# Turning the normalised latent rows with VectorE and DMAs instead of TensorE in a hybrid decoder layer

## The reference

```python
h = x @ w_in[l]
(qa, ka, va, ga, iq, ik, iw, c_q, c_kv, k_rope, gb) = _split_cols(h)
# A: rope(qa), rope(ka); indexer scores from iq, ik, iw pick 128 keys per query; softmax over these
o_a = _dsa_branch(qa, ka, va, iq, ik, iw) * jax.nn.silu(ga)
# B: latent attention; c_q has 256 columns, c_kv has 128
q  = _rmsnorm(c_q,  q_norm_g)  @ w_uq     # 8 heads of 64 + 32 rotary columns
kv = _rmsnorm(c_kv, kv_norm_g) @ w_ukv    # 8 heads of 64 key + 64 value columns
o_b = softmax(causal(q_nope k_nope + q_pe k_pe)) v * jax.nn.silu(gb)
out = jnp.concatenate([o_a, o_b], axis=-1) @ w_out[l]
x = _layernorm(DEEPNORM_ALPHA * x + out, ln_g[l], ln_b[l])
```

## Time and profile before

| | us |
|---|---|
| median of 3 runs | 284.46 (283.82 to 284.49) |
| the profiled execution | 284.04 |
| its span, from first to last instruction | 282.2 |
| TensorE busy | 273.8 (97%) |
| VectorE busy | 232.2 (82%) |
| GpSimd busy | 188.6 (67%) |
| ScalarE busy | 149.6 (53%) |
| mean granted clock of TensorE | 0.991 |

### The profile page before, as it was taken

The page is one execution under the profiler, slowest core; times in us unless marked ns, Lnnn a source line. Parts: engine busy times, 40 slices in busy tenths (PEclk is TensorE's granted clock), DMA queues, the critical chain, the costliest instruction groups (busy, mean ns, idle before and its releaser), DMA issues.

```text
span 282.2 us, 5134 instructions
## 1 busy us (share of the span) xinstructions
PE 273.8 (97%) x1664; PEld 228.6 (81%) x1664; DVE 232.2 (82%) x528; ACT 149.6 (53%) x352; POOL 188.6 (67%) x209
## 2 busy tenths in 40 slices
PE   8999999999999999999999999999999999999990
PEld 7999987778888888888888888885778788888890
DVE  2699998989999999999984798668694967986375
ACT  5656534674452576224188696777764774552000
POOL 5898999834199999999935993885799923010012
PEclk9999999999999999999999999999999999999996
DMA  7985543222623396221238652817800000545022
GB/s 240 364 256 172 151 138 130 74 77 74 149 59 93 83 250 190 74 74 44 70 91 211 231 141 78 224 53 270 349 2 2 0 1 2 172 110 168 0 77 74
DMA packets 20874, 35.41 MB, mean 125 GB/s; under 512 B 6928, under 2 KB 9488, under 8 KB 20592
## 3 DMA queue, kind: packets, MB, share of 16 engines
q1 hardware_dynamic: 20272, 34.79, 41.0%
q10 hardware_dynamic: 576, 0.29, 0.4%
HBM read 26.69 MB, written 2.10 MB: 102 GB/s over the span
## 4 chain that ended last, share of the span: by engine, by line
PE 96%; DMA 1%; DVE 1%; DVEq 0%; issue 0%; ACT 0%
PE ps L1320 52%; PE ps L1643 16%; PE ps L1560 6%; PE ps L1521 5%; PE ps L1581 3%; PE ps L1605 3%; PE ps L1503 2%; PE ps L1336 2%; PE ps L1506 2%; PE ps L1430 2%; DMA w_raw<-in_w_in 1%; PE ps L1540 1%; PE ps L1616 1%; PE ps L1439 0%; PE ps L1413 0%; DVEq L255 0%
## 5 line engine op out<-in xcount | busy, mean ns | idle before, releaser
L624 POOL TENSOR_TENSOR w_lo<-w_raw,w_hi 128x512 fp32r<-128x512 f32 (+3 forms) x62 | 83.8, 1374 | 17.4 <-ACT w_hi L770 16.8
L770 ACT ACTIVATE w_hi<-w_raw 128x512 fp32r<-128x512 f32 (+3 forms) x62 | 35.9, 595 | 55.2 <-PE ps L1320 51.9
L881 ACT ACTIVATE probs<-probs,small 128x512 f32<-128x512 f32 (+3 forms) x64 | 35.7, 559 | 23.2 <-DVE small L1150 22.8
L1643 PE MATMUL ps<-wo_hi,oT 128*128 128x512 f32 (+1 forms) x144 | 45.4, 388 | 0.0
L1320 PE MATMUL ps<-w_hi,x_lo 128*128 128x512 f32 (+3 forms) x120 | 43.0, 362 | 0.0
L1320 PE MATMUL ps<-w_lo,x_hi 128*128 128x512 f32 (+3 forms) x120 | 42.9, 361 | 0.0
L1320 PE MATMUL ps<-x_hi,w_hi 128*128 128x512 f32 x96 | 38.0, 396 | 0.0
L1320 PE MATMUL ps<-x_lo,w_hi 128*128 128x512 f32 x96 | 37.4, 390 | 0.0
L1320 PE MATMUL ps<-x_hi,w_lo 128*128 128x512 f32 x96 | 37.4, 389 | 0.0
L1320 PE MATMUL ps<-w_hi,x_hi 128*128 128x512 f32 (+2 forms) x84 | 32.1, 382 | 0.0
L1643 PEld LDWEIGHTS ps<-wo_hi,oT 128*128 128x128 f32 x144 | 25.9, 189 | 5.2 <-issue 0.2
(11 more groups left out here) (196 smaller groups left out, 631.3 us busy)
## 6 DMA issues: line engine op xcount, KB each, us to landing
w_raw<-in_w_in SPq DMA_DIRECT2D x20, 512.0 KB, 3.6
kaT_swap<-kaT SPq DMA_DIRECT2D x8, 256.0 KB, 3.8
w_raw<-in_w_out SPq DMA_DIRECT2D x4, 512.0 KB, 4.8
wo_early<-in_w_out SPq DMA_DIRECT2D x4, 512.0 KB, 4.8
wo_raw_b<-in_w_out SPq DMA_DIRECT2D x4, 512.0 KB, 4.8
x_res<-in_x SPq DMA_DIRECT2D x4, 512.0 KB, 7.1
x_raw<-in_xT SPq DMA_DIRECT2D x3, 512.0 KB, 6.4
out_y<-y SPq DMA_DIRECT2D x6, 256.0 KB, 2.4
```

Source lines behind the costliest of these rows:

```text
L624: pool.tensor_tensor(w_lo[:, s, 0:n], w_raw[:, s, 0:n], w_hi[:, s, 0:n], ALU.subtract).then_inc(w_lo_ready, 1)
L770: act.activation(dst, w_raw[:, s, 0:n], ACT.Copy).then_inc(w_hi_ready, 1)
L881: act.activation(probs[:, u % NPROBS, 0:N], probs[:, u % NPROBS, 0:N], ACT.Exp, bias=neg_max[:, u % 8:u % 8 + 1], scale=-1.0, accum_out=ro ...
L1643: ins = mm(out_ps(i, b), oT[i % 2][:, o, k, :], w[:, wcols], start=first, stop=final)
```

## The change

VectorE turns the normalised rows in 32x32 blocks, four instructions (one for 128 rows, 384 columns) after the indexer's scores and ahead of the reduction of the rotary angles, into `lat_st`. SyncE, after load 21, waits for them and issues sixteen DMAs that set the blocks in place in `lat_pT`: each takes 32 partitions to 32 partitions, with twelve runs of 128 bytes on each at the destination. TensorE's twelve transposes and their waits go. ScalarE's latT_hi and VectorE's latT_lo read `lat_pT` in SBUF where they read PSUM; latT_hi waits for the sixteen DMAs. GA's evacuation now waits for the last logits and the four turns, and TensorE's QPE for latT_hi and latT_lo. Both new tiles lie in SBUF where the raw x was.

```diff
+    lat_st = sb("lat_st", 102, [P, 4, QL_T + 1, TT, SQ])
+    lat_pT = sb("lat_pT", 108, [P, QL_T + 1, TT, 4, SQ])
...
+        def latT_raw(t):
+
+            return lat_pT[:, t].rearrange("p m a q -> p (m a q)")
...
                 load(q)
...
+                if q == LAT_PLACE_AT:
+                    sp.wait_ge(lat_turned, TT)
+                    for c in range(4):
+                        for a in range(4):
+                            sp.dma_start(lat_pT[SQ * c:SQ * (c + 1), :, :, a], lat_st[SQ * a:SQ * (a + 1), c]).then_inc(lat_placed, 16)
...
-                    act.wait_ge(side_ready, F_LAT + QL_T + 1)
+                    act.wait_ge(side_ready, F_END)
+                    act.wait_ge(lat_turned, TT)
...
             def evac_lat_hi():
                 act.wait_ge(norm_g_loaded, 32)
+                act.wait_ge(lat_placed, 16 * 16)
                 for t in range(QL_T + 1):
-                    n = F_LAT + t
-                    act.wait_ge(side_ready, n + 1)
-                    act.activation(latT_hi[:, t, :], side[:, n % 4], ACT.Copy,
+                    act.activation(latT_hi[:, t, :], latT_raw(t), ACT.Copy,
                                    scale=gq[:, t:t + 1] if t < QL_T else gkv).then_inc(lat_hi_ready, 1)
...
             dve.wait_ge(relu_used, (TT - 1) * IDX_HEADS)
 
+            dve.wait_ge(lat_normed, 2 * TT)
+            for m in range(TT):
+                V.transpose(lat_st[:, :, :, m].rearrange("p c t q -> p t c q"),
+                            lat_tok[:, m, 0:Q_LORA + KV_LORA].rearrange("p (t c q) -> p t c q", c=4, q=SQ)).then_inc(lat_turned, 1)
+
             dve.wait_ge(dve_step, rows_turns)
             reduce_angle(ang_rows[:, :], turns_rows[:, :], rows_arg_ready)
...
             for t in range(QL_T + 1):
-                n = F_LAT + t
                 dve.wait_ge(lat_hi_ready, t + 1)
-                V.scalar_tensor_tensor(out=latT_lo[:, t, :], in0=side[:, n % 4], scalar=gq[:, t:t + 1] if t < QL_T else gkv,
-                                       in1=latT_hi[:, t, :], op0=ALU.mult, op1=ALU.subtract).then_inc(side_read[n % 4], 2)
+                V.scalar_tensor_tensor(out=latT_lo[:, t, :], in0=latT_raw(t), scalar=gq[:, t:t + 1] if t < QL_T else gkv,
+                                       in1=latT_hi[:, t, :], op0=ALU.mult, op1=ALU.subtract).then_inc(lat_lo_ready, 1)
...
-            def lat_transposes():
-                pe.wait_ge(lat_normed, 2 * TT)
-                for t in range(QL_T + 1):
-                    bank = fill(F_LAT + t)
-                    for m in range(TT):
-                        ins = nc.tensor.transpose(bank[:, m * P:(m + 1) * P], lat_tok[:, m, t * P:(t + 1) * P], ident[:, :])
-                    ins.then_inc(side_ready, 1)
...
-                if g == G_V and k == KT - 1:
-                    lat_transposes()
...
-            for n in range(F_LAT, F_LAT + QL_T + 1):
-                pe.wait_ge(side_read[n % 4], seen(n) + 2)
+            pe.wait_ge(lat_hi_ready, QL_T + 1)
+            pe.wait_ge(lat_lo_ready, QL_T + 1)
...
+LAT_PLACE_AT = 21
```

More of the change, by code:

```diff
@@ L289, in build @@
         lat_ms_ready, lat_rs_ready = sem("lat_ms_ready"), sem("lat_rs_ready")
-        lat_normed, lat_hi_ready = sem("lat_normed"), sem("lat_hi_ready")
+        lat_normed, lat_hi_ready, lat_lo_ready = sem("lat_normed"), sem("lat_hi_ready"), sem("lat_lo_ready")
+        lat_turned, lat_placed = sem("lat_turned"), sem("lat_placed")
         qpe_rotated = sem("qpe_rotated")
@@ L324, in build @@
         LOGITS_USED = [sum(len(heads) for m, heads in LOGITS[:i + 1]) for i in range(len(LOGITS))]
-        F_LAT = F_LOGIT + len(LOGITS)
-        F_END = F_LAT + QL_T + 1
+        F_END = F_LOGIT + len(LOGITS)
         A_QPE = (NG - 1) * TT
```

## The result

The changed kernel takes 285.39 us (median of 15 runs, 284.75 to 287.08) beside 284.35 us of the kernel before on the same chip (15 runs): a ratio of 1.0036, 95% interval 1.0023 to 1.0050. It is slower by 1.0 us, where 1.0 us was forecast. Its profiled execution has a span of 283.0 us against 282.2.

What follows compares the result with a forecast made beforehand. TensorE, busy 97% of the span, was taken to bound the kernel. On the profiled 284.04 us, -1.1 at V and +2.1 at GB give 285.0, or 285.4 (+0.35%) on the median's footing; range 283.6 to 286.9.

Steps and rivals of the forecast that it cites:

- Twelve transposes, 1.3 us, of which 1.1 arrive: End of V: 1.3 us leave TensorE's queue, about 0.2 goes to waiting for V's first bank, gain 1.1.
- Four turns, 2.0 us: VectorE from 69.7 us: four block transposes at 0.50 each, 2.0 us, moving everything behind them by that.
- latT_lo contends beside GpSimd: VectorE: with two SBUF inputs, each latT_lo is priced like a rotary step, one per 1.70 us beside GpSimd.
- Part of it is paid back at the end of GpSimd's backlog; keys 1.85 late: VectorE: GpSimd's backlog ends at 141.0, three more steps then run at 0.62 each; keys ready 1.85 us later.
- A margin of 0.85 at GB, so 1.0 us net: GB's first bank: 1.85 us of delay less the 0.85 margin before TensorE's weight load loses 1.0 us.
- TensorE waits 2.1 us at GB and 0.2 at V: TensorE waits 2.1 us for GB's first bank and about 0.2 for V's first bank.
- My mark for being wrong: Wrong if TensorE doesn't wait at GB, or waits at GA for more than 0.5 us.
- Price zero, with this cover: SyncE's sixteen issues at 0.65 delay load 22, but cost nothing as long as it lands by 99.4 us.
- Rival 4: The wait at GB halves TensorE's clock, 2.4 to 1.2 GHz, adding 2 to 3 us: 288; chance 0.04.
- Rivals 1 to 3: 1: VectorE's delay mostly absorbed, 284.7, chance 0.16; 2: TensorE's gain arrives, 283.3, 0.11; 3: SyncE's issues too dear, 288.5, 0.12.

Runs made afterwards that it cites:

- e2: The changed kernel with latT_lo made after the keys' rotation instead of before it; 284.70 us, 1.0013 of the kernel before.
- e5: The kernel before with latT_lo's first operand taken from x's high part in SBUF instead of PSUM; 285.24 us, 1.0025 of the kernel before.
- e4: The kernel before with VectorE's four turns added, their output read by nobody; 284.15 us, 0.9993 of the kernel before.
- e1: The changed kernel with the sixteen DMAs placed behind load 19 instead of load 21; 285.43 us, 1.0048 of the kernel before.
- e11: The changed kernel with the keys' turn behind load 24 instead of load 23; 285.32 us, 1.0026 of the kernel before.
- e7: The changed kernel with VectorE's four turns made twice; 286.78 us, 1.0076 of the kernel before.
- e6: The changed kernel with the DMAs behind load 19, latT_lo in three places behind the keys' rotation, kaT copies waiting for it; 286.66 us, 1.0073 of the kernel before.
- e9: The changed kernel with the DMAs behind load 19 and ScalarE's kaT copies waiting for their own key tile alone; 283.67 us, 0.9965 of the kernel before.

## Why the prediction was right, point by point

- *Twelve transposes, 1.3 us, of which 1.1 arrive.* Right: the four kernels with the early placing gain 0.95 to 1.13 at V.
- *Four turns, 2.0 us.* Right: 1.96.
- *latT_lo contends beside GpSimd.* Right: 1.77 each against 0.74 without it (e2), and e5 shows that the operand's place alone makes it. The rule of the Trainium skill (SBUF — State Buffer, "Who interferes with whom"), that a VectorE instruction with two SBUF inputs contends with a GpSimd instruction that reads SBUF, holds here. Its further part, that the second waits for the whole of the other, would give more than the 1.70 us a step that was measured: a VectorE step alone took 0.69 and a GpSimd split alone 1.29.
- *Part of it is paid back at the end of GpSimd's backlog; keys 1.85 late.* Right: 1.55 as read, 1.78 counted from each trace's own offset, in both traces of the changed kernel. The turns' part was priced too high, 0.8 for 0.4 (e4), since the bias write, which gave 0.4 back, was not in the count; latT_lo's was priced too low, 1.05 (1.85 less 0.8) for 1.54 (e5). The two misses cancel in part.
- *A margin of 0.85 at GB, so 1.0 us net.* Right: 1.78 late and 0.92 arrived leave 0.86. Two small errors cancel in it. ScalarE frees the first of four full banks after 0.52 us (four in 2.07) and not 0.64, which held TensorE's own pace; and the weight load stands 0.19 behind the free bank (151.00 for 150.81), not at it.
- *TensorE waits 2.1 us at GB and 0.2 at V.* Wrong in its parts: the products waited 0.3 and 1.4 (0.6 and 1.2 in the second trace). My mark for being wrong, over 0.5 us of wait at GA, was met. The step that failed is "Price zero, with this cover". An issue came as priced (0.67 us), but load 22 landed at 99.6, 0.2 past the cover of 99.4, and I looked only at it. Load 23, no longer spaced from it by 6.4 us but by 1.5, and with the keys' turn at its heels, took 7.3 us to land instead of 4.1. The sum survived, because what is lost at V comes off the wait at GB (e1, e11). The prediction says this of TensorE's gain, that it is only a longer wait; that a loss there would be covered too it did not work out, and e7 shows where it ends: 3.0 us lost at V, with no wait left at GB to take them.
- *Rival 4*, a wait at GB that costs more than itself through the clock, was given 0.04 and was nearer than that. The clock stayed at full behind e1's wait, 1.68 us between products, and fell at 2.07 (e6) and 2.71 (e7).
- *Rivals 1 to 3.* The delay was not absorbed; TensorE's gain did not arrive (it does in e9); sixteen issues at 0.67 helped to make the wait at V, but did not cost time. The Trainium skill's table and rule that the prediction sets beside the issues (DMA: Bandwidth & Descriptors, "Anatomy of one DMA — SWDGE (gpsimd) path" and "Bandwidth") stand there under DMAs that GpSimd issues; these came from SyncE.

## What to carry to other kernels

Work taken off the bound engine is worth only what the next late arrival leaves of it: here some 1.0 us of the transposes' 1.1 arrived once the sixteen DMAs stood early and ScalarE's wait was cut down to the tile it needs, an edit that is worth nothing in the kernel before. With waits in one line, the one that looks longest in the trace need not be the one that sets the time; undo one at a time and see whether the other grows. Before an operand is moved from PSUM to SBUF, look at what GpSimd does at that time, and before small DMAs are put ahead of a load, look at the landing of the loads behind it and not only at its issue.

## What the runs showed of the hardware that was not expected

- TensorE's clock fell to half for 3.4 us with single waits of 2.07 us (e6) and 2.71 us (e7) in a stream without gaps, not with 1.44 and 1.68 us (changed, e1). In e6 it fell 0.8 us after the work had resumed, in e7 0.4 us before; it cost 1.5 and 1.4 us on top of the wait.
- A DMA of 32 partitions with twelve runs of 128 bytes each took 0.62 us to issue, 0.67 apart, and 2.1 to land; one with a single 2 KB run per partition takes 0.59. Twelve times the runs cost 5% more of the issue.
- A 512 KB load landed after 7.0 to 7.3 us where it had another load 1.5 us ahead of it and four DMAs of 256 KB right behind it, and after 4.3 and 4.4 with only one of the two (e1, e11).
- Two microseconds more on VectorE, which had no gap for 72 us, came out as 0.4 us at its end (e4): 1.1 came back behind the end of GpSimd's backlog at 141 us, 0.4 at the bias write.
